# A two-layer block and what follows, on one core: the first two layers in another order of work

## The reference

```python
def hybrid_layer(x, c, cos, sin, pre_g, post_g, w_ada, b_ada, w_in, w_out):
    mod = jnp.einsum('bd,de->be', jax.nn.silu(c), w_ada) + b_ada
    shift, scale, gate = jnp.split(mod, 3, axis=-1)
    h = rms_norm(x, pre_g) * (1 + scale[:, None, :]) + shift[:, None, :]
    proj = jnp.einsum('bsd,de->bse', h, w_in)            # 1024 -> 4096
    qa, ka, va, ga, qb, kb, vb, gb = jnp.split(proj, SPLIT_POINTS, axis=-1)
    # q and k get a rotary embedding on 16 of 64 features of each head
    o_a = merge(dilated_mixture_attention(qa, ka, va)) * jax.nn.silu(ga)   # 8 heads
    o_b = merge(moba_attention(qb, kb, vb)) * jax.nn.silu(gb)              # 8 heads
    y = jnp.einsum('bse,ed->bsd', jnp.concatenate([o_a, o_b], axis=-1), w_out)
    return x + gate[:, None, :] * rms_norm(y, post_g)
```

## Time and profile before

| what | us |
|---|---|
| median of 3 runs | 1761.97 (1760.56 to 1765.05) |
| the profiled execution | 1762.42 |
| its span, first to last instruction | 1760.6 |
| first product of layer 0 begins | 24.82 |
| first product behind layer 1 begins | 392.18 |

### The profile page before, as it was taken

One profiled execution on the slowest core, in us unless ns is written; L12 is line 12 of the kernel. 1 busy time (PEld: TensorE's weight loads), 2 busy tenths in 40 slices (PEclk: granted clock), 3 DMA queues, 4 the chain that ended last, 5 costly groups with the idle time before them and its releaser, 6 DMA issues. The chain is left out here.

```text
span 1760.6 us, 22621 instructions
## 1 busy us (share of the span) xinstructions
PE 1656.4 (94%) x8918; PEld 1400.0 (80%) x8918; DVE 1189.9 (68%) x2104; ACT 703.2 (40%) x1090; POOL 64.4 (4%) x96
## 2 busy tenths in 40 slices
PE   5999988989999999989987999999999999999998
PEld 4676767677888888878774789987999878889986
DVE  6877888666886666457456677776777568565554
ACT  3555443453222122234444453335334355354332
POOL 1000100000000000010001000000000010010000
PEclk9989998999999999999998999999999999999999
DMA  9756574433556666332221158874877677455551
GB/s 382 286 182 198 170 289 160 144 120 117 208 201 222 209 220 215 115 103 93 96 73 60 62 223 303 307 289 155 292 245 267 225 278 250 143 180 182 187 173 46
DMA packets 93050, 337.61 MB, mean 192 GB/s; under 512 B 10624, under 2 KB 11136, under 8 KB 92688
## 3 DMA queue, kind: packets, MB, share of 16 engines
q1 hardware_dynamic: 90704, 328.11, 53.2%
q0 software_dynamic: 2240, 8.06, 1.4%
HBM read 335.08 MB, written 1.05 MB: 191 GB/s over the span
## 5 line engine op out<-in xcount | busy, mean ns | idle before, releaser
L296 ACT ACTIVATE sb_hi<-sb_w 128x1024 fp32r<-128x1024 f32 x428 | 430.8, 1052 | 284.8 <-DMA sb_w<-in_w 231.3
L290 PE MATMUL bank<-sb_hTh,sb_hi 128*128 128x256 f32 (+1 forms) x1280 | 396.5, 310 | 0.0
L290 PE MATMUL bank<-sb_hTl,sb_hi 128*128 128x256 f32 (+1 forms) x1280 | 396.2, 309 | 0.0
L290 PE MATMUL bank<-sb_hi,sb_hTh 128*128 128x512 f32 x640 | 266.8, 417 | 24.9 <-DVE sb_hTh L317 14.5
L290 PEld LDWEIGHTS bank<-sb_hTh,sb_hi 128*128 128x128 f32 x1280 | 244.4, 191 | 12.5
L290 PEld LDWEIGHTS bank<-sb_hTl,sb_hi 128*128 128x128 f32 x1280 | 244.4, 191 | 12.5
L290 PE MATMUL bank<-sb_hi,sb_hTl 128*128 128x512 f32 x640 | 240.9, 401 | 0.6 <-POOL sb_hTl L299 0.6
L290 PEld LDWEIGHTS bank<-sb_hi,sb_hTh 128*128 128x128 f32 x640 | 125.6, 196 | 63.7 <-issue 23.3
L310 DVE CUSTOM_DVE_ANT_0 sb_w<-sb_w,sb_cb 128x1024 f32<-128x1024 f32 x144 | 175.1, 1219 | 0.0
L290 PEld LDWEIGHTS bank<-sb_hi,sb_hTl 128*128 128x128 f32 x640 | 124.9, 195 | 29.5 <-POOL sb_hTl L299 1.4
L296 ACT ACTIVATE sb_sg<-bank 128x512 f32<-128x512 f32 (+2 forms) x65 | 35.9, 563 | 219.2 <-PE bank L290 218.5
(11 more groups left out here) (470 smaller groups left out, 3444.0 us busy)
## 6 DMA issues: line engine op xcount, KB each, us to landing
sb_w<-in_w SPq DMA_DIRECT2D x428, 512.0 KB, 4.3
sb_w<-in_mw SPq DMA_DIRECT2D x192, 512.0 KB, 4.4
sb_G<-in_na_rpb POOLq DMA_DIRECT2D x16, 96.0 KB, 2.4
sb_X<-in_x SPq DMA_DIRECT2D x1, 1024.0 KB, 7.8
sb_cb<-in_cvec POOLq DMA_DIRECT2D x2, 512.0 KB, 9.3
sb_XC<-in_ctx POOLq DMA_DIRECT2D x1, 1024.0 KB, 7.8
sb_arena<-in_sg_ln_g POOLq DMA_DIRECT2D x1, 1024.0 KB, 7.1
sb_arena<-in_sg_ln_b POOLq DMA_DIRECT2D x1, 1024.0 KB, 10.4
```

Source lines behind the costliest of these rows:

```text
L290: return self.e.matmul(out, a, b, start=start, stop=stop)
L296: return self.e.activation(out, a, f, **kw)
```

## The change

- **High parts.** A second table `HSPLIT`, with lead 4 in place of 3, gives ScalarE's steps; the low parts keep `SPLIT`, lead 3. In `m00` and behind it up to the mixer a ninth high buffer is used.
- **Vectors behind heads.** In the two layers VectorE does the low part, then the head, then the step's vector tile (`dve_vectors`). In the stream a vector tile of these layers is asked for with key `t` and not `t - 2`.
- **Heads.** All copies of turned probabilities are ScalarE's, ahead of the step's exponentials; so are all copies of turned `q` and `k`. Outputs of four heads go side by side to bank 7, and VectorE scales them in one instruction at steps `i` = 6 and 10, with one reciprocal for four heads. Scores and turned probabilities take turns in banks 4 to 6 (`HB3`).
- **Four kinds.** The first 16 tiles are the four quarters of `q`, `k`, `v` and of `q` of attention `b`; the stream's groups have 4 and 4 tiles. ScalarE alone makes the modulated input of layer 0 and its high part, VectorE its low part.
- **Steps.** Attention A of layer 0 begins at step 15 (14 before), B at 23 (25), one step each; in layer 1 A begins at 10 (11), and tiles 36 and 37 are done for all tokens at once.
- **The start.** `x` is asked for first, the constants in two pieces, the two other condition vectors (`CB[1]`, `CB[2]`), the mask and the context by GpSimd only after tiles 5 and 13. VectorE makes half of the first squares; the rotary tables stand ahead of the first vector. The rotary embedding takes 3 instructions in place of 6.
- **Banks.** `m00` begins in banks 4 to 7 in place of 0 to 3, its first norm in 0 to 3.

```diff
-        if l == 0:
-            for k in range(0, 8, 2):
-                for kind in "qkv":
-                    rows("w_in", (l,), k, k + 2, BASE1[kind])
+        if l == 0:
+            for k in range(0, 8, 2):
+                for kind, g in (("q", 0), ("k", 0), ("v", 0), ("q", 1)):
+                    rows("w_in", (l,), k, k + 2, BASE1[kind] + g * 2048)
...
-    for first, last, count in ((12, 35, 24), (40, 66, 24), (W_F00 + 4, W_MX - 10, 64), (W_F01 + 4, W_F10 - 10, 32),
+    for first, last, count in ((16, 35, 24), (40, 66, 24), (W_F00 + 4, W_MX - 10, 64), (W_F01 + 4, W_F10 - 10, 32),
...
-def split_times():
+def split_times(lead):
...
-        ahead = max([3] + [min(t - h + 11, 7, h + 3 - t) for h in ends if h - 8 < t <= h])
+        ahead = max([lead] + [min(t - h + 11, 7, h + 3 - t) for h in ends if h - 8 < t <= h])
...
-SPLIT = split_times()
+HSPLIT, SPLIT = split_times(4), split_times(3)
...
-    rest += [(t - 2, 1, ("m", n)) for t, ns in VT.items() for n in ns]
+    rest += [(t - 2 * (t >= W_F00), 1, ("m", n)) for t, ns in VT.items() for n in ns]
...
+            e.dma(X[:, :, :], I["x"].rearrange("(j p) d -> p j d", p=128)).then_inc(LD["x"].sem, LD["x"].put("x", by=16))
             e.dma(CB[0][:, :], I["cvec"][0:1, :].partition_broadcast(128)).then_inc(LD["cb"].sem, LD["cb"].put(0, by=16))
-            e.dma(X[:, :, :], I["x"].rearrange("(j p) d -> p j d", p=128)).then_inc(LD["x"].sem, LD["x"].put("x", by=16))
+            e.dma(posi[:, :], I["positions"][:, :]).then_inc(LD["pos"].sem, LD["pos"].put(0, by=16))
             for n, item in enumerate(ORDER):
+                if n == 0:
+                    e.dma(cst[:, 0:138], I["consts"][:, 0:138]).then_inc(LD["cst"].sem, LD["cst"].put(0, by=16))
...
         def pe_attention(e, l, g, i):
...
-                b = BANK["O", l, g, h] = TB.take()
-                for f in b.free():
-                    e.wait_ge(*f)
+                b = bank[7]
+                if h % 4 == 0:
+                    for f in b.free():
+                        e.wait_ge(*f)
...
+        def act_attention(e, l, g, i):
+            if 2 <= i <= 9:
+                h = i - 2
+                e.wait_ge(*done(TRP, "P", l, g, h))
...
+                e.act(PT[h % 3], BANK["P", l, g, h].ap[:, 0:384], ACT.Copy).then_inc(AE.sem, AE.put("PT", l, g, h))
             if i < 8:
...
-            if i >= 3:
-                h = i - 3
-                b, yc = BANK["O", l, g, h], slice(g * 512 + h * 64, g * 512 + h * 64 + 64)
...
-                for j in range(2):
-                    m = e.ts(y[:, j, yc], b.ap[:, j * 64:j * 64 + 64], stat[:, l, g, h, 2 + j:3 + j], None, ALU.mult)
+            if i in (6, 10):
+                q = i // 4 - 1
+                r = stat[:, l, g, q * 4:q * 4 + 4, 2:4]
+                e.wait_ge(*done(EX, l, g, q * 4 + 3))
+                e.recip(r, r).then_inc(DE.sem, DE.put("recip", l, g, q))
...
+                e.wait_ge(*done(PVS, l, g, q * 4 + 3))
...
+                e.tt(y[:, :, c].rearrange("p j (h d) -> p j h d", d=64),
+                     bank[7].ap[:, :].rearrange("p (j h d) -> p j h d", j=2, h=4),
+                     r.rearrange("p h j -> p j h").unsqueeze(3).to_broadcast([128, 2, 4, 64]), ALU.mult).then_inc(
+                         DE.sem, DE.put("O", l, g, q))
...
         def pool_start(e):
+            pool_rstd(e, "a0")
+            e.wait_ge(*done(USED, 5))
+            e.dma(blk.rearrange("p a b -> p (a b)"), I["blk"][:, :]).then_inc(LD["blk"].sem, LD["blk"].put(0, by=16))
+            e.wait_ge(*done(USED, 13))
...
-            ALLB.i = 0
+            ALLB.i = 4 * (ns == 2)
+            AB.i = 0
```

269 lines of the change are left out of this document (136 added, 133 removed), and 2 rows, old and new, of the table B1.

## The result

The changed kernel takes 1695.41 us (median, 1693.04 to 1698.74) against 1763.51 (1760.56 to 1765.55) in the same comparison: ratio 0.9616, 95% interval 0.9593 to 0.9639. The profiled execution took 1695.14, its span is 1693.4.

A forecast was written before the change was run, and what follows sets the result against it. TensorE was busy 94%, so time could be won only where it waits or runs at its lower clock. Gains of 4.8 + 5.0 + 11.5 + 22.3 + 5.4 = 49.0 us from 1762.4 gave 1713, range 1701 to 1738.

The forecast's parts named there:

- Part 1, start: Before the first product: x, constants and first weight tile arrive earlier, so the first product comes 4.8 us earlier.
- Part 2, first sums: First sums of layer 0: with four kinds TensorE no longer waits for VectorE; 5.0 us taken of 5.7.
- the deduction of 0.7: First sums: 5.7 us lowered to 5.0 because VectorE's margin of 0.7 in 11 is thin.
- Parts 3 and 4, the heads: Heads of layers 0 and 1: idle time and lost clock go, 11.5 us of 14.4 and 22.3 of 27.9.
- I take four fifths: Heads of both layers: share of the possible gain counted, as one or two waits stay at the output projection.
- The token that goes back and forth: Layer 1 heads: VectorE and ScalarE wait on each other in a loop of 6.08 us against TensorE's work of 4.77.
- four remedies: Heads: fewer VectorE instructions, copies ahead of exponentials, high parts one tile earlier, masks ahead of the vector tile.
- Part 5, the bank: Behind layer 1: TensorE's wait of 5.34 us for a bank and 1.6 of half rate can go; 5.4 taken.
- The edits at nothing: Later stages: high lead 4 changes only ScalarE's order, low parts keep their lead; counted as no gain.
- VectorE as the bound: Rival, first sums and heads: VectorE takes over as bound, heads bring half; 1727.5, up to 1738; chance 0.27.
- The shared bank: Rival, heads: TensorE waits at every fourth head until VectorE has read bank 7; 44 us, 1757; chance 0.05.
- Tiles too late: Rival, layers: tiles land late, some 44 head steps wait 1.5 us each, 66 us, 1779; chance 0.04.

The follow-up runs named there:

- e12_pool_loads: Changed kernel with GpSimd's loads of the other condition vectors, mask and context at the very start, not held back: 1702.38 us, ratio 0.9648.
- e6_vectors_lead3: Changed kernel with, in the two layers, the vector tile ahead of the head again and high lead 3: 1734.24 us, ratio 0.9830.
- e7_copies: Changed kernel with copies of turned probabilities as before: even heads' on ScalarE behind the exponentials, odd heads' on VectorE behind the masks: 1697.81 us, ratio 0.9623.
- e13_bank0_norm4: Changed kernel with m00's products beginning in banks 0 to 3 and its first norm in banks 4 to 7, as before: 1702.16 us, ratio 0.9662.
- e2_lead3_later: Changed kernel with high lead 4 in the two layers alone, lead 3 and eight high buffers from m00 on: 1706.84 us, ratio 0.9693.

## Why the prediction was right in direction and short by 18 us

- **Part 1, start**: 4.8 forecast, 5.8 measured. `x` at 5.63 and the constants at 7.86 came as forecast. Mis-sized was the term of the rotary tables, taken as 3.3 from the earlier trace rows; they took 10.14 - 7.86 = 2.3. GpSimd's loads are shown to be 2.7 of the gain (`e12_pool_loads`); the rest is argued from the rows.
- **Part 2, first sums**: 5.0 of a possible 5.7 forecast, 6.8 measured. No wait was left, so the deduction of 0.7 was wrong; the other 1.1 I can't place. Three kinds give back 3.0, so the fourth kind is under half of this part. That they would cost 2 to 5 was expected from VectorE's group; the waits came at ScalarE's input (1.22 and 1.34), and how VectorE's lag gets there was not followed.
- **Parts 3 and 4, the heads**: the step that failed is "I take four fifths", twice. Its reason, one or two waits where the heads meet the output projection, came from no row, and no such wait came. All of part 3's 14.4 went (14.7), and all of part 4's 27.9 (28.3). After's rows show why nothing stays: with the loop open there is no next late engine, VectorE's step is 3.99 against TensorE's 4.77. The two bounds were low by 0.3 and 0.4.
- My reason for the gain was half right. The token that goes back and forth was the cause (`e6_vectors_lead3` brings it back with 38 us); but I gave four remedies, and either of two is enough. The copies of probabilities cost nothing where they were (`e7_copies`); those of turned `q` and `k` stay untested.
- **Part 5, the bank**: 5.4 forecast, 7.2 measured from `m00`'s first product (5.65 in the stretches as cut above, since I took the seventh for the first). Mis-sized was "I leave 1.5 for it": no wait of that size for the first norm came, and all of the 6.9 went. 5.4 come back with the old bank (`e13_bank0_norm4`).
- **The edits at nothing**: "the change leaves its work as it is" was the second step that failed. The mixer took 13.3 us less: by the rows shown the two kernels stand 965.02 - 893.22 = 71.80 apart near its end, and (759.93 - 2.95) - (698.67 - 0.19) = 58.50 before it. I had costed the high lead by ScalarE's load, 514 of 1368, and named as its cover that low parts keep their lead. But what TensorE waits for there is a norm that stands behind high and low parts in both queues, and lead and buffer move these out of its way; undoing both gives back 11 to 14 us (`e2_lead3_later`). Against it go 6.6 us for the arena's products behind the heads (1608 x 4.1 ns) and 2.05 that I did not trace: 13.3 - 6.6 - 2.05 = 4.65.
- **The edge** between the layers: 0 forecast, -0.2.
- **Rivals**: VectorE as the bound didn't come (116.90 and 140.30 of TensorE busy). The shared bank didn't: among after's waits is none for `sb_XN` in the heads; the bank is guarded as a whole at every fourth head, and here that costs nothing. Tiles too late didn't either: ScalarE's waits for weight tiles in layer 1, 8.5 us in 7 places with 2.8 the longest, never reach TensorE, busy 140.30 of 140.30.

Of the 18.2 us missed against the sum of 49.0, 8.5 are the fifth left out of parts 3 and 4, 0.7 what the heads gave beyond their bounds, 4.65 the later stages, 1.8 the first sums, 1.8 the bank and 1.0 the start, less 0.2 at the edge.
